# Where the two parts of a shift vector stand in the moving rows of a two-block transformer kernel

## The reference, cut to what matters

```python
mod = (cond @ ada_w[i] + ada_b[i])[:, None, :]
sh1, sc1, g1, sh2, sc2, g2 = jnp.split(mod, 6, axis=-1)
h = rmsnorm_2(x, norm1_g[i]) * (1.0 + sc1) + sh1
... attention: qkv = h @ w_qkv ...
h = rmsnorm_2(x, norm2_g[i]) * (1.0 + sc2) + sh2
x = x + g2 * swiglu_2(h, w_gate[i], w_up[i], w_down[i])
```

## Time and profile before

| | us |
|---|---|
| median of three runs | 1131.81 |
| the profiled execution | 1131.81 |
| its span, first to last instruction | 1130.0 |
| TensorE busy | 1119.1 (99%) |
| VectorE busy | 894.8 (79%) |
| ScalarE busy | 638.2 (56%) |
| GpSimd busy | 106.6 (9%) |

### The profile page before, as it was taken

How to read it: one execution, slowest core, us unless ns; L and a number is a source line. 1 busy time by engine, 2 the same in 40 slices (tenths; PEclk the granted TensorE clock), 3 DMA queues, 4 the chain that set the end, 5 groups by cost and what they waited for, 6 DMA issues and landing times.

```text
span 1130.0 us, 23720 instructions
## 1 busy us (share of the span) xinstructions
PE 1119.1 (99%) x9668; PEld 1094.4 (97%) x9668; DVE 894.8 (79%) x1533; ACT 638.2 (56%) x1070; POOL 106.6 (9%) x146
## 2 busy tenths in 40 slices
PE   8999999999999999999999999999999999999999
PEld 8999999998899999999997899999999999999998
DVE  5989997565658999998989898878768887955642
ACT  6744555445555655555567666445458876744531
POOL 2000002011100100001423710000100002000000
PEclk9999999999999999999999999999999999999999
DMA  8787998654445699998842348889654444666651
GB/s 291 270 299 265 334 342 297 205 164 135 122 160 180 223 327 337 334 319 329 280 120 88 113 151 294 286 291 340 226 184 148 133 131 136 219 209 197 195 180 62
DMA packets 70668, 251.92 MB, mean 223 GB/s; under 512 B 7840, under 2 KB 9504, under 8 KB 70432
## 3 DMA queue, kind: packets, MB, share of 16 engines
q1 hardware_dynamic: 70560, 250.41, 66.1%
HBM read 249.33 MB, written 1.05 MB: 222 GB/s over the span
## 4 chain that ended last, share of the span: by engine, by line
PE 93%; DVE 4%; POOL 1%; DMA 1%; SPq 0%; issue 0%; ACT 0%; POOLq 0%; DVEq 0%
PE ps L566 29%; PE ps L570 28%; PE ps L567 28%; PE ps L704 1%; DVE s L1487 1%; DVE wlo L1076 1%; PE ps L561 1%; PE ps L560 1%; PE ps L557 1%; PE ps L739 1%; POOL ss L2093 1%; DVE s L1499 1%; PE ps L751 1%; PE ps L1013 1%; PE ps L998 1%; DMA raw<-w_stream 1%
## 5 line engine op out<-in xcount | busy, mean ns | idle before, releaser
L566 PE MATMUL ps<-hhi,whi 128*128 128x256 f32 (+1 forms) x1944 | 544.2, 280 | 0.9 <-DVE gu L1210 0.8
L570 PE MATMUL ps<-hhi,wlo 128*128 128x256 f32 (+1 forms) x1944 | 540.3, 278 | 0.7 <-DVE wlo L1076 0.7
L567 PE MATMUL ps<-hlo,whi 128*128 128x256 f32 (+1 forms) x1944 | 540.2, 278 | 0.0
L1076 DVE TENSOR_TENSOR wlo<-raw,whi 128x1024 fp32r<-128x1024 f32 x371 | 454.9, 1233 | 42.3 <-ACT whi L1682 41.6
L1682 ACT ACTIVATE whi<-raw 128x1024 fp32r<-128x1024 f32 x371 | 385.8, 1053 | 76.1 <-DMA raw<-w_stream 42.2
L566 PEld LDWEIGHTS ps<-hhi,whi 128*128 128x128 f32 x1944 | 366.2, 188 | 6.3 <-issue 4.9
L570 PEld LDWEIGHTS ps<-hhi,wlo 128*128 128x128 f32 x1944 | 366.3, 188 | 0.9 <-DVE wlo L1076 0.9
L567 PEld LDWEIGHTS ps<-hlo,whi 128*128 128x128 f32 x1944 | 366.3, 188 | 0.1
L566 PE MATMUL ps<-hidhi,whi 128*128 128x256 f32 x704 | 194.3, 276 | 0.0
L567 PE MATMUL ps<-hidlo,whi 128*128 128x256 f32 x704 | 194.3, 276 | 0.0
L570 PE MATMUL ps<-hidhi,wlo 128*128 128x256 f32 x704 | 194.3, 276 | 0.0
(11 more groups left out here) (242 smaller groups left out, 1258.6 us busy)
## 6 DMA issues: line engine op xcount, KB each, us to landing
raw<-w_stream SPq DMA_DIRECT2D x371, 512.0 KB, 4.6
raw<-ada_in SPq DMA_DIRECT2D x96, 512.0 KB, 5.0
raw<-w_stream SPq DMA_DIRECT2D x6, 256.0 KB, 4.9
con<-con_in SPq DMA_DIRECT2D x1, 1089.5 KB, 7.2
out_dram<-vx SPq DMA_DIRECT2D x8, 128.0 KB, 3.9
vx<-x_in SPq DMA_DIRECT2D x2, 256.0 KB, 5.6
cond<-c_in SPq DMA_DIRECT2D x1, 512.0 KB, 7.4
vx<-x_in SPq DMA_DIRECT2D x3, 128.0 KB, 4.5
```

What stands on the lines that cost most here:

```text
L566: e.matmul(bank, wh, r_hi, start=i == FIRST[o] and not shared, stop=False, skip_group_check=True)
L567: e.matmul(bank, wh, r_lo, start=False, stop=False, skip_group_check=True)
L570: mm = e.matmul(bank, wl, r_hi, start=False, stop=i == LAST[o], skip_group_check=True)
L1076: e.tensor_tensor(ring(wlo, n), raw[:, slot, :], ring(whi, n).bitcast(F32), ALU.subtract).then_inc(lo_done, 1)
```

## The change

Both parts of the shift now stand in hhi: its high part in column 256, its low part in column 257. hlo's columns 256 and 257 keep the zeros of the start. PSUM column 256 thus ends as the high part's product, column 257 as the low part's, and whoever copied column 256 sums the two. The product with hlo moves 256 columns instead of 258 in mix2, in mix3 and in the first seven chunks of ffn2 and ffn3; the eighth chunk of these two keeps 258, and so do the tiles of ffn0. The products with hhi keep 258 everywhere. The bias copy becomes a multiply by ones with an accumulated sum over the two columns (both_parts), which writes the product into a small scratch tile and the sum into the bias; in scale_gu two such instructions stand for one copy. The shift tile has half its size, and padding keeps all other tiles at their addresses. The memset of the shift tile at the start is gone.

```diff
-        shift = sb("shift", [P, 2, 2, KD, 2])
+        shift = sb("shift", [P, 2, 2, KD])
+        sb("gap_t", [P, 2 * 2 * KD])
...
-        sb("gap_s", [P, 40])
+        both = sb("both", [P, 16, 2])
+        sb("gap_s", [P, 8])
...
-                        e.matmul(bank, wh, r_lo, start=False, stop=False, skip_group_check=True)
+                        e.matmul(bank[:, 0:r_lo.shape[1]], wh, r_lo, start=False, stop=False, skip_group_check=True)
...
-            def normed(s, n, anew=False):
+            def normed(s, n, anew=False, m=S):
...
-                    return hhi[:, kt, 0:n], hlo[:, kt, 0:n]
+                    return hhi[:, kt, 0:n], hlo[:, kt, 0:m]
...
                 if n > 1:
-                    tiles(c0 + 8 * CH, begin, operand)
+                    tiles(c0 + 7 * CH, begin, operand)
+                    tiles(c0 + 8 * CH, begin, normed(s, S + 2, m=S + 2))
                     operand = normed(s, S, True)
...
-                e.tensor_copy(shift[:, layer, half, :, 0], mod[:, layer, o:o + KD]).then_inc(mod_ok, 1)
+                e.tensor_copy(shift[:, layer, half, :], mod[:, layer, o:o + KD]).then_inc(mod_ok, 1)
...
-                e.tensor_tensor(hlo[:, :, S:S + 2], shift[:, layer, half, :, :], hhi[:, :, S:S + 2].bitcast(F32), ALU.subtract).then_inc(sh_lo, 1)
+                e.tensor_tensor(hhi[:, :, S + 1], shift[:, layer, half, :], hhi[:, :, S].bitcast(F32), ALU.subtract).then_inc(sh_lo, 1)
+
+            both_no = itertools.count()
+
+            def both_parts(dst, pair, scale=1.0):
+
+                e.tensor_tensor_reduce(both[:, next(both_no) % 16, :], pair, k("ones", 0, 2), scale, 0.0, ALU.mult, ALU.add, dst)
...
                 if n > 1:
-                    e.tensor_copy(bcol[:, b, :], ps[:, p:p + 2, S])
+                    for j in range(2):
+                        both_parts(bcol[:, b, j:j + 1], ps[:, p + j, S:S + 2])
...
-                    e.tensor_copy(bias, bank[:, S:S + 1])
+                    both_parts(bias, bank[:, S:S + 2])
...
-                    e.tensor_scalar(st3[:, b, j:j + 1], bank[:, S:S + 1], HD ** -0.5 if w[0] == "q" else 1.0, None, ALU.mult)
+                    both_parts(st3[:, b, j:j + 1], bank[:, S:S + 2], HD ** -0.5 if w[0] == "q" else 1.0)
...
-            v_step.mark(e.memset(shift[:], 0.0))
...
-                e.activation(hhi[:, :, S:S + 2], shift[:, layer, half, :, :], ACT.Copy).then_inc(sh_hi, 1)
+                e.activation(hhi[:, :, S], shift[:, layer, half, :], ACT.Copy).then_inc(sh_hi, 1)
```

More of the change, by code:

```diff
@@ L1 @@
+import itertools
 from contextlib import ExitStack
```

## The result

The changed kernel takes 1136.55 us (median of nine runs, 1135.64 to 1143.13) against 1131.82 before (nine runs, 1131.39 to 1132.22): ratio 1.0047, interval 1.0031 to 1.0064. It is slower by 4.7 us, where 2.5 us less had been forecast, and it lies outside the range. Some executions of nearly every kernel timed here, the one before included (6 of 31 in one series), are about 7 us longer than the rest, and where such a one was profiled it lost them before 222 us, upstream of the change; so the table further down gives the median of the lower group, the executions without that loss.

The account below looks back on a forecast made before the run. TensorE was taken to bound the kernel everywhere but mix2's second half, where VectorE does. 1131.81 us less 2.57 for short products plus 0.10 for pair sums gave 1129.3 us, range 1127.9 to 1132.2.

Parts of the forecast that it names:

- The pace downstream: Rival, chance 0.12: tiles behind ffn2's or ffn3's eighth chunk turn slow, 3.8 us lost, 2.3 more with the down stage.
- ffn2 leaves the long rows fast: Ground against slow tiles behind ffn2's eighth chunk: only four products after the long rows are not fast.
- the eighth chunk, which lies right in front, is left as it is: Ground against a slow pace in ffn2: the long chunk directly before the pure 256-column rows is not edited.
- The price of a short product: Products with hlo in mix2, mix3, ffn2, ffn3: each shortened one gains 7.3 ns, 352 of them 2.57 us.
- half the price: Rival, chance 0.30: short products in mixed rows run at 117.4 ns, not 113.0; gain 1.0 us less 0.1, 1130.9 us.
- Two columns for two: Rival, chance 0.04: short hlo products save only two columns' clock time, 0.3 us in all, giving 1131.6 us.
- Pair sums: VectorE's bias sums: 0.02 to 0.03 us over a copy; five in mix2's second half lose 0.10 us, at most 0.75.
- The first half of mix2: Sign: mix2 up to its first score product should shorten by 0.35 us.
- VectorE's chain: Rival, chance 0.07: in mix2, meetings with GpSimd's product appear or vanish, 0.49 us each; could lose 1.5 us, 1130.8.
- Memset: Start of the kernel: dropping its 0.11 us, in front of a 2.08 us wait for the first rows, gains nothing.
- shift steps: ScalarE's copy and VectorE's subtraction, four of each, move 8 elements per partition instead of 16: nothing gained.
- covered sums in ffn2 and mix3: VectorE's extra 0.5 us per ffn stage and 0.7 us in mix3 are hidden and cost nothing; uncovered, 0.5 per ffn stage.

Follow-up runs that it names:

- e1: Changed kernel with hlo products at 258 columns in all eight first chunks of ffn2 and ffn3; 1131.03, 1131.14, 1137.66, 1137.86 us.
- e3: Changed kernel with every hlo product back at 258 columns, leaving both shift parts in hhi and the pair sums; 1131.72 us, ratio 1.0000.
- e7: Changed kernel with short hlo products in the eighth chunks too, nudges kept; five runs 1129.77 to 1130.72 us, five 1136.80 to 1137.94.
- e4: Changed kernel with ffn2's eighth chunk at its regular place in the weights' ring, not 16 bytes lower; 1129.99, 1130.61, 1130.67, 1137.17 us.
- e9: Changed kernel with ffn2's sums product one tile later (after 23 tiles, not 22); nine runs 1129.63 to 1130.57 us, one 1137.63.
- e8: Kernel before the change with ffn2's eighth chunk at its regular place in the ring; seven of ten runs 1131.69 to 1132.45 us, others 1139.05 to 1139.23.
- e6: Changed kernel with no nudge in ffn2 and ffn3 and short hlo products in their eighth chunks; eight runs 1129.38 to 1130.53 us, two 1136.91 and 1137.29.
- e12: Changed kernel, short eighth chunks, no nudges in ffn2 and ffn3, sums after 23 and 22 tiles; nine runs 1129.72 to 1131.04 us, three 1137.36 to 1137.45.
- e10: Changed kernel with ffn3's sums product one tile earlier (after 22 tiles, not 23); 1142.81 us, ratio 1.009.

## Why the prediction was wrong

**The step that failed** is one that the sum took as nothing: that the pure 256-column rows behind ffn2's eighth chunk would keep their pace. They went from 340 to 353 ns per tile and kept that through down2, 1392 products, and lost 6.16 us, against 1.6 us gained. The prediction had this as its rival "The pace downstream" and priced it well: 3.8 us, and 2.3 more with the down stage, 1135.4. With the smaller gain that was measured this gives 1131.8 + 6.2 - 1.6 = 1136.4, and 1136.55 came. What was wrong is its weight of 0.12 and that the range left it out, on two grounds. One, that ffn2 leaves the long rows fast, took the outcome of one arrangement for a property of the stage. The other, "the eighth chunk, which lies right in front, is left as it is", was no protection: that chunk, long and nudged, is fast behind long rows (e1, e3) and slow behind mixed ones. e1, e7, e4 and e9 each take one condition away, and each is fast there. No row of before told the two outcomes apart, so nothing supported so small a chance, and the range should have reached past 1135.

**The price of a short product** was put at 7.3 ns and measured less. mix3, the longest clean stretch: 192 tiles start from 828.0 to 917.2 before and from 833.8 to 922.1 after, by these rows:

```profile
L567 PE MATMUL ps<-hlo,whi x192: 278/283/289, 828.0 to 917.2; 128*128 128x258 f32 x192
```

```profile
L571 PE MATMUL ps<-hlo,whi x192: 277/282/288, 833.8 to 922.1; 128*128 128x256 f32 x192
```

89.2 - 88.3 = 0.9 us, 4.9 ns per tile with the 0.95 of the finer comparison. Over all stretches 1.6 us came for 2.57, so this term of the sum was right in sign and too large by 1.0 us. The price lies between the forecast (7.3) and "half the price" (2.9): a mixed row does not give each product its own pace but takes the two-tile pattern above, with a mean of 357 ns per tile, where 354 had been forecast and 358 for the rival. The short product's 282 ns is neither of the two paces of pure rows.

**Two columns for two**, 0.8 ns per product, is ruled out: 4.9 ns were gained for two columns. With it goes the formula that the prediction took from the Trainium skill (TensorE: Matmul & The Clock Gate, "Back-to-back issue gap") as an account of this step. The section itself calls it the gap of an isolated matmul and says that in a stream of weight loads and matmuls, as here, both set the spacing; the prediction left that out.

**Pair sums** started the next operation 0.08 us later, the lower end of the forecast, and e3 finds no cost of the whole part. The first half of mix2 gave 0.21 us for a forecast of 0.35. Its second half gave 0.04 back, where 0.10 had been allowed; e8, which has no pair sums, shows the same 0.04 there, so not even the sign of that term is shown. With no more than this moving in that stretch, VectorE's chain as a rival did not occur. Memset, shift steps and the covered sums in ffn2 and mix3 cost nothing that shows.

Not settled: why a nudged long chunk locks from one tile of the pattern and not from the other, why without the nudge the fast pace follows with no lock, and what in the engine makes the two paces. Nor is it shown where the executions of the changed kernel at 1143 lost their 6.5 us; in the kernels profiled in their longer group (e1, e6, e7, e12) it was before 222 us.

## What to carry to other kernels

Where rows of identical matmuls run at two paces in one trace, a change to what stands in front of a long row can be worth what the row's length makes of it (here 1392 products, 6.2 us) and not what the edit itself saves (1.6 us). Give both outcomes a real chance in the forecast. If the outcome is the bad one, the gain may still be there: shift an interruption by one tile (e9), or give the special chunk the place or the columns of its neighbours (e4, e7), and time again. Set the n-th instruction of one trace beside the n-th of the other: the step in the difference names the place.

## What had not been expected of the hardware

- Pure rows of 256-column products run at 340 or 353 ns per tile of three, at the same full granted clock, and keep that pace through a change of operand, stage and buffer: from 670 to 833 us here, 163.9 us.
- Behind mixed rows and a nudged long chunk, which of the two is taken changed with the number of tiles behind an interruption: 33 fast, 34 slow, in both stages, 6.2 us each (e9, e10). No other number was run, so that it is the parity is inferred from the two-tile pattern. It changed too with a place in SBUF that differs by 16 bytes (e4).
- Rows of 258, 256, 258 columns took neither pace, but 353 and 361 ns in turn; in the nudged chunks of e7 they settled at 360 (121, 123, 116).
- The same code took either pace in ffn0 and down0, which no edit touches: 353 ns per tile in the traces of e1, e6, e7 and e12, 340 in all others. Executions of one kernel differ by the same 7 us (3 of 12 of e12 are the longer ones). The longer runs of the kernel before, 6 of 31, fit this but have no trace.
- A multiply with an accumulated sum over two PSUM columns takes as long as a copy of one, 152 ns on average against medians of 150 and 158, and its accumulator read of 80 ns lies beside the next operation.
